# Who takes the low parts of sixteen weight chunks during a bit search: the vector engine or GpSimd

## Chip, cores and metric

One core of one Trainium2 chip. The metric is the device time of one execution in microseconds (us). Engines are named as in the profile: PE is TensorE (matmul), PEld its weight load, DVE the vector engine, ACT the scalar engine, POOL is GpSimd, SP is SyncE, which here issues most DMAs.

## What is computed

One step of a decoder layer for 272 prompt tokens (16 learned ones and 256) and 32 sample tokens (8 sequences of 4). The model is 2048 wide. The part of the reference that matters here is the sparse attention of the sample tokens: an indexer scores all 2048 + 4 past keys, and each query attends only to its best 256.

```python
h = einsum('btd,de->bte', x, w_in)          # q, k, v, iq, ik, iw, p
score = sum_h w[t,h] * relu(iq[t,h] . ik[s])
_, idx = lax.top_k(score, 256)              # per query
a = softmax(q . k[idx]) v[idx]
m = pooled(p) @ w_pool * pool_scale
x = layer_norm(ALPHA * x + concat(a, m) @ w_out)
f = (silu(gate) * val) @ w_down             # gate, val: conv of x @ w_up
y = layer_norm(ALPHA * x + f)
```

Everything is float32. The output must keep float32's accuracy and, above all, the same keys must be chosen.

## The kernel before, in words

**Weights as chunks, each in two parts.** All weights stream through three slots of 128x1024 float32 (`RING = 3`, 512 KB a chunk), in 354 chunks. For each chunk n: SP loads it into `raw` (`load_chunk`, L330 to L350) once `lo_done` says that the chunk three before it has been split; ACT rounds it to the matmul's reduced format, `w_hi = raw` (`hi`, L1012 to L1018), once TensorE is through with the chunk three before (`chunk_used`); then `w_lo = raw - w_hi` is formed (`lo`, L1348 to L1353) by DVE, and TensorE does three products for each 128x128 block, hi*x_hi, hi*x_lo and lo*x_hi (L459 to L461), 24 matmuls a chunk. `hi_done`, `lo_done` and `chunk_used` are counters: each chunk adds one, in order.

**The order of the work is written out by hand.** The stretch in question is a loop of 32 steps, one for each chunk KS + i (KS = 26), i = 0 to 31, which every engine's program goes through in its own way. The chunks are the projections to k, p and v. While TensorE multiplies chunk KS + i, ACT and DVE prepare chunk KS + i + 2, and each engine puts other work into the step:

- TensorE (L629 to L687): the chunk; in steps 4 to 7 the prompt's index scores (`prompt_index`); the sample scores against the cached keys, `sample_scores` (L609), one unit of four pages in most steps, two in steps 12, 15, 18 and on; and `total` (L588 to L593), a matmul with a 0/1 matrix that sums a count over partitions. In steps 4 to 19 `total` stands twice in each step: ahead of the last quarter of the chunk's matmuls ("mid"), and at the end of the step.
- DVE (L1560 to L1648): in steps 4 to 19 the search for the threshold. All 544 scores of each partition lie in `sc`. A candidate's bits are settled from the top down, 32 of them: `count` (L1505 to L1508) counts the scores at or over the candidate in one instruction with an accumulator, TensorE's `total` sums the counts, and `next_bit` (L1510 to L1516) sets the candidate anew in three instructions on 128x1, the last of them `cand = cand xor flip_i` (L1516). One round of this at a time can be under way. Two rounds go into each step, and between them stood `lo(KS + 2 + i)`.
- Also on DVE: `index_head` (L1489 to L1499), the weighted sum over the prompt's index heads, two heads in each of the steps 4 to 7 (four instructions with two tensor inputs); `rope_key` in steps 9, 11, 13 and 15 (a shuffle and three products, L1359 to L1362), each behind the second count of its step.
- ACT (L1109 to L1150): `hi(KS + 2 + i)` at the head of each step, then relus, evictions and score copies.
- SP (L384 to L407): the chunk load, then one or two units of cached keys (four loads of 256 KB each), which wait for `k_used`.
- GpSimd (L944 to L966): at the start memsets and 80 loads of cached index keys, the last at about 80 us; then it waits for `p_acc` (the last `index_head`) and masks the prompt's scores with three `affine_select` (L962), which `prompt_top` reads in steps 28 and on; then it issues half of the value loads (L966), the first at about 290 us. Between 80 and 290 us it has nothing else.

**Behind the search**, in step 20, DVE splits chunk KS + 22 and finishes the mask (L1598 to L1609); TensorE waits there for one more count (L634).

Of the kernel before, what the change touches and what calls it, by code (L numbers as in the profile page):

```python
# [37 lines left out]
KS, PS, VS = 26, 34, 50  # L38
# [34 lines left out]
def slot_of(n):  # L73

    return n % RING
# [22 lines left out]
def layer(nc, xT, w_iq, w_ik, w_in, w_out, w_up, w_down, kT_cache, v_cache, ik_cache, pages,  # L98
# [3 lines left out]
    f32, f32r, i32 = mybir.dt.float32, mybir.dt.float32r, mybir.dt.int32  # L102
    ALU, ACT, AX = mybir.AluOpType, mybir.ActivationFunctionType, mybir.AxisListType
# [9 lines left out]
    def put(name, shape, dt=f32, where=None):  # L113
        if where is None:
            where = region(4 * int(np.prod(shape[1:])))
        return nc.alloc_sbuf_tensor_at(name, shape, dt, offset=where)
# [9 lines left out]
    raw = put("raw", [128, RING, CK * CW])  # L126
    w_hi = put("w_hi", [128, RING, CK * CW], f32r)
    w_lo = put("w_lo", [128, RING, CK * CW], f32r)
# [88 lines left out]
    with ExitStack() as ctx:  # L217
# [3 lines left out]
        def sem(name):  # L221
            return ctx.enter_context(nc.semaphore(name))
# [12 lines left out]
        hi_done, lo_done, chunk_used = sem("hi_done"), sem("lo_done"), sem("chunk_used")  # L235
# [45 lines left out]
        def page_numbers(engine, first):  # L281

            return nc.values_load_multi_w_load_instructions(pt_sb[0:1, first:first + UNIT], engines=[engine],  # L283
                                                            min_val=0, max_val=NPHYS - 1)[1]
# [658 lines left out]
        @block.gpsimd  # L943
        def _(pool):  # L944
            PL = mybir.EngineType.Pool
            pool.memset(ones[:], 1.0).then_inc(preset, 1)
            pool.memset(tiny[:], EPS).then_inc(preset, 1)
            pool.memset(sc[:], NEG).then_inc(preset, 1)
            pool.memset(cand[:], 2.0).then_inc(preset, 1)
            pool.memset(q_pad[:], 0.0).then_inc(preset, 1)  # L950
            pool.memset(p_score[:, 0:64], 0.0).then_inc(preset, 1)
            pool.wait_ge(pages_in, 16)
            for g, b in [(0, b) for b in range(DB)] + [(1, 0), (1, 1)]:
                for j in range(2):
                    for i, r in enumerate(page_numbers(PL, NPG * b + 8 * j + 4 * g)):
                        pool.dma_start((ik_a, ik_b)[g][64 * j:64 * j + 64, b, i, :],
                                       ik_cache[bass.ds(r, 1)].rearrange("a p n -> p (a n)")).then_inc(ik_in[2 * g], 16)
            pool.wait_ge(p_acc, IH)
            pool.wait_ge(preset, 6)
            for i, (t0, n, keys, col) in enumerate(PQ):  # L960
                view = p_score[0:n, col:col + keys]
                pool.affine_select(out=view, in_=view, pattern=[[-1, keys]], compare_op=ALU.is_ge,  # L962
                                   fill=NEG if i else -FAR, base=t0, channel_multiplier=1).then_inc(p_causal, 1)

            for u in range(1, 32, 2):
                load_value_unit(pool, PL, u)  # L966

            def centre(z, tmp, blocks, round_):

                pool.wait_ge(mean_kept, round_ + 1)  # L970
                for k in blocks:
                    pool.tensor_tensor(z[:, k], z[:, k], tmp[:, 0], ALU.subtract).then_inc(centred, 1)  # L972

            centre(z1[:, :, M0:T], ln_a, CENTRE[0], 0)
            pool.wait_ge(x1_lo, KB)
            pool.wait_ge(rows_out, 32)
            pool.wait_ge(v_out, 16)
            pool.wait_ge(p_out, 16)
            for i in range(NUP):

                for a in range(2):
                    if i:
                        pool.wait_ge(conv_v, i * 4)
                    pool.wait_ge(conv_in, 32)
                    src = c_state[:, 2 * i + FB * a:2 * i + FB * a + 2, 0:16].rearrange("p j (b w) -> p j b w", w=2)
                    dst = u_ext[:, 2 * a:2 * a + 2, PT:PT + 6 * DB].rearrange("p j (b w) -> p j b w", w=6)
                    pool.tensor_copy(dst[:, :, :, 0:2], src).then_inc(ctx_put, 1)  # L987

                flat = c_state[:].rearrange("p j w -> p (j w)")
                for a in range(2):  # L990
                    pool.wait_ge(g_free, i * 4 + (4 * SL_UP + 2 * a + 2))
                    pool.wait_ge(ctx_put, i * 2 + 2)
                    dst = flat[:, i * 36 + 18 * FB * a:i * 36 + 18 * FB * a + 36].rearrange("p (j b w) -> p j b w", b=9, w=2)
                    src = u_ext[:, 2 * a:2 * a + 2, PT - 2:PT + 52].rearrange("p j (b w) -> p j b w", w=6)
                    pool.tensor_copy(dst, src[:, :, :, 0:2]).then_inc(tail_put, 1)  # L995

            pool.wait_ge(h_split, 2 * NUP)
            pool.wait_ge(tail_put, 2 * NUP)
            for k in range(KB):
                pool.tensor_tensor(z2[:, k], x_hi[:, k, META:T].bitcast(f32), x_lo[:, k, META:T].bitcast(f32),  # L1000
                                   ALU.add).then_inc(residual, 1)
            centre(z2, ln_b, CENTRE[1], 1)
# [329 lines left out]
        def _(dve):  # L1332
# [15 lines left out]
            def lo(n):  # L1348
                c = slot_of(n)
                width = 8 * IKW if IK0 <= n < Q0 else CK * CW  # L1350
                dve.wait_ge(hi_done, n + 1)
                dve.tensor_tensor(w_lo[:, c, 0:width], raw[:, c, 0:width], w_hi[:, c, 0:width].bitcast(f32),  # L1352
                                  ALU.subtract).then_inc(lo_done, 1)  # L1353
# [24 lines left out]
            def rope_key(j):  # L1378
                dve.wait_ge(g_free, 4 * SL_K + j + 1)
                if j:  # L1380
                    dve.wait_ge(k_roped, j)
                rope(k_t[0:32, j], rope_q, partner_q, k_roped)
# [177 lines left out]
            for i in range(32):  # L1560
# [17 lines left out]
                if 4 <= i < 20:  # L1578
                    it = 1 + 2 * (i - 4)
                    if it > 1:  # L1580
                        next_bit(32 - it)
                    count(cand[:], ALU.is_ge, it)
                    lo(KS + 2 + i)
                    next_bit(31 - it)
                    if it < 31:
                        count(cand[:], ALU.is_ge, it + 1)
                    else:
                        then(dve.tensor_scalar(sc[:], sc[:], sign, None, ALU.mult))
                        then(dve.tensor_scalar(thr, cand[:], sign, None, ALU.mult))
                        count(thr, ALU.is_gt, 32)  # L1590
# [2 lines left out]
                    index_head(2 * (i - 4) + 1)  # L1593
                if i in (9, 11, 13, 15):
                    rope_key((i - 9) // 2)
                if i >= 20:
                    lo(KS + 2 + i)
                if i == 20:  # L1598
# [246 lines left out]
            for s in range(NDN):  # L1845
                end = DN0 + DNC * (s + 1)
                for n in range(done, min(end + 2, END)):
                    lo(n)
                    c = n - DN0 - DNC
# [116 lines left out]
```

## Time and profile before

| | |
|---|---|
| median of 3 runs | 1372.3 us (1371.9, 1372.3, 1377.79) |
| the profiled execution's own time | 1376.97 us |
| its span on the core | 1375.3 us |
| PE busy | 1329.3 us, 97% |
| DVE busy | 772.4 us, 56% |
| ACT busy | 599.3 us, 44% |
| POOL busy | 169.5 us, 12% |
| mean granted clock of TensorE | 0.989 |

The profiled execution is one of the slower ones shown: its time lies 4.7 us over the median. Busy times and spans are those of that one execution. A matmul's end is modelled in the profile, so a busy PE is not PE at its peak. The clock is given as a share of 2.4 GHz. A wait for several semaphores is put down to the one that came last. Idle time of an engine costs nothing where another one sets the pace.

### The profile page before, as it was taken

To read this page: it belongs to the slowest core of one execution; us is meant where nothing else is said; L and a number is where in the kernel's file an instruction comes from. 1 tells how busy PE (TensorE), PEld (TensorE's weight loads), DVE (VectorE), ACT (ScalarE), POOL (GpSimd) and SP (SyncE) were. 2 spreads that over 40 slices of the span, in tenths; PEclk is the share of its full clock that TensorE was granted. 3 is DMA by queue.
4 is the path that set the end of the run, shared out by engine and by line. 5 is a ranking of instruction groups with operands and counts; after the bars stand their busy time and mean duration, and the time that the engine had idled before them with its cause. 6 is when DMAs were issued, how large, how long until landed. Compare 5 with 4: busy or idle time off the path is not lost.

```text
span 1375.3 us, 25589 instructions
## 1 busy us (share of the span) xinstructions
PE 1329.3 (97%) x9824; PEld 1225.8 (89%) x9824; DVE 772.4 (56%) x1291; ACT 599.3 (44%) x964; POOL 169.5 (12%) x286
## 2 busy tenths in 40 slices
PE   6999998999999999999999999999999999999995
PEld 6977776677677989999999999999999999999995
DVE  4645877766444766565565565565565535443434
ACT  3343312343333367554554554554554433333434
POOL 5510000012230040010010010010010500000002
PEclk9999999999999999999999999999999999999998
DMA  9656789989987536556555555555555655555552
GB/s 254 191 171 230 258 303 368 306 288 340 319 318 270 140 106 191 162 157 178 163 158 170 169 156 169 167 160 170 162 166 171 181 169 161 158 169 156 166 162 76
DMA packets 97421, 272.70 MB, mean 198 GB/s; under 512 B 13097, under 2 KB 19570, under 8 KB 97042
## 3 DMA queue, kind: packets, MB, share of 16 engines
q1 hardware_dynamic: 89618, 251.65, 59.1%
q0 software_dynamic: 7680, 19.41, 4.2%
q8 instruction: 77, 1.26, 0.4%
q14 instruction: 46, 0.38, 0.1%
HBM read 265.83 MB, written 5.18 MB: 197 GB/s over the span
## 4 chain that ended last, share of the span: by engine, by line
PE 82%; DMA 5%; SPq 5%; DVE 4%; issue 3%; ACT 1%; POOLq 0%; ACTq 0%; DVEq 0%; POOL 0%
PE G L459 25%; PE G L460 24%; PE G L461 24%; DMA raw<-in_w_in 2%; PE A L778 2%; SPq L283 1%; SPq L298 1%; PE A L609 1%; SPq L376 1%; DVE w_lo L1352 1%; DMA raw<-in_w_iq 1%; DMA raw<-in_w_out 1%; DMA k_ring<-in_kT_cache 1%; ACT w_hi L1018 1%; DMA v_ring_x<-in_v_cache 1%
## 5 line engine op out<-in xcount | busy, mean ns | idle before, releaser
L1352 DVE TENSOR_TENSOR w_lo<-raw,w_hi 128x1024 fp32r<-128x1024 f32 x354 | 434.9, 1229 | 451.9 <-ACT w_hi L1018 450.8
L1018 ACT ACTIVATE w_hi<-raw 128x1024 fp32r<-128x1024 f32 x354 | 373.9, 1056 | 566.1 <-PE G L461 459.1
L459 PE MATMUL G<-x_hi,w_hi 128*128 128x290 f32 (+1 forms) x1856 | 560.0, 302 | 17.7 <-DVE w_lo L1352 14.0
L460 PE MATMUL G<-x_lo,w_hi 128*128 128x290 f32 (+1 forms) x1856 | 554.3, 299 | 0.0
L461 PE MATMUL G<-x_hi,w_lo 128*128 128x290 f32 (+1 forms) x1856 | 550.9, 297 | 0.0
L459 PEld LDWEIGHTS G<-x_hi,w_hi 128*128 128x128 f32 x1856 | 351.4, 189 | 27.8 <-issue 21.5
L460 PEld LDWEIGHTS G<-x_lo,w_hi 128*128 128x128 f32 x1856 | 353.2, 190 | 0.2
L461 PEld LDWEIGHTS G<-x_hi,w_lo 128*128 128x128 f32 x1856 | 351.0, 189 | 0.0
L461 PE MATMUL G<-h_hi,w_lo 128*128 128x288 f32 x704 | 208.7, 296 | 0.0
L459 PE MATMUL G<-h_hi,w_hi 128*128 128x288 f32 x704 | 208.6, 296 | 0.0
L460 PE MATMUL G<-h_lo,w_hi 128*128 128x288 f32 x704 | 205.3, 292 | 0.0
L460 PEld LDWEIGHTS G<-h_lo,w_hi 128*128 128x128 f32 x704 | 134.2, 191 | 0.1
L459 PEld LDWEIGHTS G<-h_hi,w_hi 128*128 128x128 f32 x704 | 132.2, 188 | 1.4 <-issue 1.4
L461 PEld LDWEIGHTS G<-h_hi,w_lo 128*128 128x128 f32 x704 | 131.9, 187 | 0.0
L1806 DVE SCALAR_TENSOR_TENSOR conv<-u_ext,cp_sb,conv 128x304 f32<-128x304 f32 x176 | 90.2, 533 | 44.1 <-ACT conv L1303 40.9
L995 POOL COPY c_state<-u_ext 128x36 f32<-128x36 f32 x44 | 11.4, 260 | 369.3 <-ACT u_ext L1291 369.2
L987 POOL COPY u_ext<-c_state 128x32 f32<-128x32 f32 x44 | 39.4, 926 | 135.8 <-DVE conv L1806 118.6
L1303 ACT ACTIVATE conv<-u_ext,cp_sb 128x304 f32<-128x304 f32 x88 | 51.5, 638 | 0.0
L1290 ACT ACTIVATE u_ext<-G 128x258 f32<-128x258 f32 x88 | 33.7, 383 | 16.8 <-PE G L461 14.2
L972 POOL TENSOR_TENSOR z<-z,ln_b 128x288 f32<-128x288 f32 x10 | 8.7, 904 | 262.3 <-ACT ln_b L1257 262.3
L459 PE MATMUL G<-a_hi,w_hi 128*128 128x290 f32 x128 | 38.7, 302 | 2.3 <-DVE z L1798 1.4
L459 PE MATMUL G<-m_hi,w_hi 128*128 128x290 f32 x128 | 40.3, 315 | 0.0
(293 smaller groups left out, 1172.4 us busy)
## 6 DMA issues: line engine op xcount, KB each, us to landing
raw<-in_w_up SPq DMA_DIRECT2D x176, 512.0 KB, 3.6
raw<-in_w_down SPq DMA_DIRECT2D x88, 512.0 KB, 3.6
k_ring<-in_kT_cache SPq DMA_DIRECT2D x128, 256.0 KB, 4.1
raw<-in_w_in SPq DMA_DIRECT2D x48, 512.0 KB, 5.7
raw<-in_w_out SPq DMA_DIRECT2D x32, 512.0 KB, 5.4
v_ring_x<-in_v_cache POOLq DMA_DIRECT2D x44, 256.0 KB, 5.7
v_ring_p<-in_v_cache SPq DMA_DIRECT2D x32, 256.0 KB, 5.0
v_ring_x<-in_v_cache SPq DMA_DIRECT2D x28, 256.0 KB, 4.5
```

Source lines behind the costliest of these rows:

```text
L283: return nc.values_load_multi_w_load_instructions(pt_sb[0:1, first:first + UNIT], engines=[engine], min_val=0, max_val=NPHYS - 1)[1]
L298: eng.dma_start(k_ring[:, UNIT * (u % 4) + i, :], kT_cache[bass.ds(r, 1)].rearrange("a p n -> p (a n)")).then_inc(k_in[u % 4], 16)
L459: pe.matmul(out, hi, xh, start=start, stop=False)
L460: pe.matmul(out, hi, xl, start=False, stop=False)
L461: return pe.matmul(out, lo, xh, start=False, stop=stop)
L778: mm = pe.matmul(A[32 * i:32 * i + 32, 2, :], p_tok[:, b // 4, b % 4, UNIT * u + i, :], value_slot(w, i), start=u == 0, stop=u == 3)
L987: pool.tensor_copy(dst[:, :, :, 0:2], src).then_inc(ctx_put, 1)
L1018: act.activation(w_hi[:, c, 0:width], raw[:, c, 0:width], ACT.Copy).then_inc(hi_done, 1)
L1290: act.activation(u_ext[:, j, 0:PT], G[:, j, 0:PT], ACT.Copy).then_inc(act_own, 1)
L1303: act.activation(conv[:, j, 0:UO], u_ext[:, j, 0:UO], ACT.Identity, scale=cp_sb[:, t, 0:1], bias=cp_sb[:, t, 3:4]).then_inc(conv_a, 1)
L1352: dve.tensor_tensor(w_lo[:, c, 0:width], raw[:, c, 0:width], w_hi[:, c, 0:width].bitcast(f32), ALU.subtract).then_inc(lo_done, 1)
L1806: return dve.scalar_tensor_tensor(out=conv[:, j, 0:UO], in0=u_ext[:, j, w:w + UO], scalar=cp_sb[:, t, w:w + 1], in1=conv[:, j, 0:UO], op0= ...
```

## The change

GpSimd forms w_lo of chunks KS + 6 to KS + 21, those that DVE formed in steps 4 to 19. It does so in one run behind its loads of index keys and ahead of the masking of the prompt's scores; each split waits for its w_hi alone, the first also for the six splits before it by DVE, so that `lo_done` counts in order. In step 20 DVE waits for all of GpSimd's splits before its own next one.

```diff
@@ gpsimd
                         pool.dma_start((ik_a, ik_b)[g][64 * j:64 * j + 64, b, i, :],
                                        ik_cache[bass.ds(r, 1)].rearrange("a p n -> p (a n)")).then_inc(ik_in[2 * g], 16)
+            for n in range(KS + 6, KS + 22):
+                c = slot_of(n)
+                if n == KS + 6:
+                    pool.wait_ge(lo_done, n)
+                pool.wait_ge(hi_done, n + 1)
+                pool.tensor_tensor(w_lo[:, c, :], raw[:, c, :], w_hi[:, c, :].bitcast(f32), ALU.subtract).then_inc(lo_done, 1)
             pool.wait_ge(p_acc, IH)
             pool.wait_ge(preset, 6)
@@ vector, steps 4 to 19
                     count(cand[:], ALU.is_ge, it)
-                    lo(KS + 2 + i)
                     next_bit(31 - it)
@@ vector
                     rope_key((i - 9) // 2)
+                if i == 20:
+                    dve.wait_ge(lo_done, KS + 22)
                 if i >= 20:
                     lo(KS + 2 + i)
```

## Rows read from the trace of the kernel before

**Rows 1.** The page: busy us of an engine, share of the span, instructions.
```profile
PE 1329.3 (97%) x9824; PEld 1225.8 (89%) x9824; DVE 772.4 (56%) x1291; ACT 599.3 (44%) x964; POOL 169.5 (12%) x286
```

**Rows 2.** Busy time by stretch: busy us of each engine, granted clock, DMA.
```profile
136.00:236.00 100.00, 91.66 (x647) 70.95 (x647) 77.98 (x221) 26.57 (x41) 0.88 (x3) 0.98 0.86 304
...
184.40:188.40 4.00, 4.00 (x19) 4.00 (x20) 3.76 (x10) 1.06 (x1) 0.00 (x0) 0.58 1.05 388
...
236.00:240.00 4.00, 4.00 (x34) 2.31 (x34) 3.11 (x5) 0.43 (x1) 0.00 (x0) 0.57 1.02 383
...
236.00:400.00 164.00, 162.88 (x1157) 116.15 (x1160) 95.19 (x247) 58.62 (x115) 27.93 (x52) 0.99 0.91 312
```

**Rows 3.** Who waited for whom, 137 to 234 us: total, times, longest.
```profile
PE A L593 <- DVE junk L1507: 5.6, 10, 2.4
```

**Rows 4.** Groups of DVE, 137.9 to 232 us: busy, mean ns, idle before.
```profile
L1507 DVE TENSOR_SCALAR_CACHE_REDUCE junk<-sc,cand 128x544 f32<-128x544 f32 x31 | 24.2, 779 | 1.1
L1352 DVE TENSOR_TENSOR w_lo<-raw,w_hi 128x1024 fp32r<-128x1024 f32 x16 | 19.6, 1225 | 7.0 <-ACT w_hi L1018 6.6
```

**Rows 5.** Timeline: start, us, engine and line, idle before and its releaser.
```profile
136.35 0.38 PE L593 MATMUL A<-sel_k,msum 128*128 128x1 f32 x2 [1.58 <-DVE junk L1507]
...
180.48 1.06 ACT L1018 ACTIVATE w_hi<-raw 128x1024 fp32r<-128x1024 f32 x1 [9.04 <-DMA raw<-in_w_in]
...
181.64 1.23 DVE L1352 TENSOR_TENSOR w_lo<-raw,w_hi 128x1024 fp32r<-128x1024 f32 x1 [2.91 <-ACT w_hi L1018]
...
184.25 0.38 PE L593 MATMUL A<-sel_k,msum 128*128 128x1 f32 x2 [2.40 <-DVE junk L1507]
...
235.73 0.38 PE L593 MATMUL A<-sel_k,lmat 128*128 128x1 f32 x2 [1.58 <-DVE sc L1601]
```

**Rows 6.** Timeline of step 6.
```profile
148.12 1.06 ACT L1018 ACTIVATE w_hi<-raw 128x1024 fp32r<-128x1024 f32 x1
...
149.95 0.16 DVE L1516 TENSOR_TENSOR cand<-cand,flip_i 128x1 int32<-128x1 int32 x1
...
150.99 0.38 PE L593 MATMUL A<-sel_k,msum 128*128 128x1 f32 x2
```

**Rows 7.** Timeline of step 10.
```profile
170.38 1.06 ACT L1018 ACTIVATE w_hi<-raw 128x1024 fp32r<-128x1024 f32 x1 [4.27 <-PE G L461]
...
171.87 0.46 DVE L1361 TENSOR_TENSOR k_t<-k_t,rope_q 32x304 f32<-32x304 f32 x1
...
174.21 0.38 PE L593 MATMUL A<-sel_k,msum 128*128 128x1 f32 x2
```

**Rows 8.** Timeline of steps 13 and 17.
```profile
189.93 1.06 ACT L1018 ACTIVATE w_hi<-raw 128x1024 fp32r<-128x1024 f32 x1 [4.43 <-PE G L461]
...
192.55 0.16 DVE L1516 TENSOR_TENSOR cand<-cand,flip_i 128x1 int32<-128x1 int32 x1
...
214.43 1.06 ACT L1018 ACTIVATE w_hi<-raw 128x1024 fp32r<-128x1024 f32 x1 [3.31 <-DMA raw<-in_w_in]
...
216.05 0.16 DVE L1516 TENSOR_TENSOR cand<-cand,flip_i 128x1 int32<-128x1 int32 x1
...
217.96 0.28 PE L593 MATMUL A<-sel_k,msum 128*128 128x1 f32 x2
```

**Rows 9.** Timeline where GpSimd and DVE meet.
```profile
161.87 0.88 POOL L962 TENSOR_SCALAR_AFFINE_SELECT p_score<-p_score 50x64 f32<-50x64 f32 x3 [82.48 <-DVE p_score L1498]
...
161.98 0.78 DVE L1516 TENSOR_TENSOR cand<-cand,flip_i 128x1 int32<-128x1 int32 x1
...
1080.78 1.34 DVE L1352 TENSOR_TENSOR w_lo<-raw,w_hi 128x1024 fp32r<-128x1024 f32 x1 [0.63 <-ACT w_hi L1018]
```

**Rows 10.** One line's instructions: duration ns least/median/most, first and last start.
```profile
L1000 POOL TENSOR_TENSOR z<-x_hi,x_lo x16: 805/816/1812, 1080.2 to 1096.6; 128x288 f32<-128x288 f32 x16
...
L995 POOL COPY c_state<-u_ext x44: 213/216/313, 532.6 to 1070.6; 128x36 f32<-128x36 f32 x44
...
L1460 DVE MAX8 top<-p_score x2: 324/379/434, 289.0 to 310.7; 104x8 f32<-104x168 f32 x1, 104x8 f32<-104x272 f32 x1
```

## The prediction

> **What bounds the kernel now.** I read the page first: TensorE is busy 97% of the span [rows 1]. So a change on the vector engine pays only where TensorE waits for it. Next the busy time by stretch: over 136 to 236 us, where the 32 bits of the threshold are searched, TensorE is busy 91.66 of 100 us, DVE 77.98 and GpSimd 0.88; right after its two longest idle times there are 4 us at a granted clock of 0.58 and 0.57, the lower level of 1.2 GHz [rows 2]. The waits put 5.6 us of that idle time on the count of the search (L593 behind L1507) [rows 3]; the timeline shows its largest piece, 2.40 us at 184.25, because the vector engine sat 2.91 us in front of the split w_lo until ACT had made w_hi and only then came back to the search, and behind it 1.58 us more at 235.73, in step 20, after DVE's split of chunk 48 [rows 5]. Together 7.2 us.
>
> The search is a ring: DVE counts (L1507, 779 ns [rows 4]), TensorE sums over partitions (L593), DVE flips the bit in three small instructions, the last of them cand = cand xor flip_i (L1516). It goes round twice in each step i = 4 to 19: TensorE asks for one count in front of the last quarter of the chunk ("mid") and one at the end of the step.
>
> **The change, part by part.** *Removed from DVE:* sixteen splits of 1225 ns, 19.6 us [rows 4], and DVE's waits for w_hi in front of them. They lie beside TensorE's work, except where TensorE then waits. Most that can come back is those 7.2 us and the two slow stretches. Their price: 4 us at 0.58 lose 0.42 x 4 = 1.7 us, 3.4 for both [rows 2]. Ceiling: 7.2 + 3.4 = **10.6 us**.
>
> *Added on GpSimd:* sixteen splits of 128x1024. The trace has no such size. Nearest rows: two-input operations of 128x288, least 805, median 816 ns [rows 10]. In proportion that is 1024/288 x 816 = 2.90 us, the upper end; taking 213 ns of it as fixed, what GpSimd's copies of 36 elements need at least [rows 10], leaves 603/288 = 2.1 ns an element, so 213 + 1024 x 2.1 = 2.36. I take **2.45 us**, nearer to the second, since a large operation has its fixed part once, and keep 2.2 to 2.9. The Trainium skill (GPSIMD Engine Reference, "Elementwise — side-by-side cycle accounting") gives 4497 ns for 2048 elements, by which a split would be an estimated 2.25 us and the sum some 2 us smaller; no run here shows that size. GpSimd has room: 2.45 us in a step of some 6, and TensorE uses a chunk two steps after its w_hi. So w_lo is not late itself, and the raw slots, freed by lo_done, come free no later than now: today DVE splits after its first count. Cost of that: nothing, covered by two steps of lead; without the cover 1.2 us a chunk. GpSimd's queue: the three affine selects move from 161.87 to behind the last split, about 230; their first reader starts at 289.0 [rows 10], so 59 us cover them. The value loads behind them wait for k_used and stay where they are. No DMA moves; SP's waits are on the same counts. The added DVE wait at step 20 is for work done before w_hi of chunk 48, for which DVE waits anyway.
>
> *What it puts in the way: the lock.* At 161.87 GpSimd ran three selects in 0.88 us, up to 162.75. DVE's cand, which takes 159 ns otherwise, started at 161.98 and took 0.78, up to 162.76 [rows 9]. So DVE's tiny two-input operation waited until GpSimd was done. The same at 1080.78: w_lo took 1.34 us beside a run of GpSimd's two-input operations [rows 9], and of these, 816 ns by the median, one took 1812 [rows 10]: held in its turn. The Trainium skill (SBUF — State Buffer, "SBUF: two separate sides") has the rule: whichever comes first, GpSimd or a DVE operation with two SBUF inputs, holds the shared ports for its whole instruction. The trace agrees. Counting itself has one tensor input, and at 779 ns for 544 elements I take it to run beside GpSimd; no row here shows that overlap.
>
> So each GpSimd split is a closed window for cand, for the three products of a rope, and for the index heads. It opens 1.16 us after w_hi starts (DVE's own split began so much after it at 181.64 against 180.48, [rows 5]) and lasts 2.45. Against each step's ring:
>
> - *Steps 5 to 7, behind the index heads.* Step 6: w_hi at 148.12, window 149.3 (149.6 behind the running head) to 152.05. cand stood at 149.95, is held 2.1 us, and the count with it; TensorE wanted it at 150.99, when it was just done [rows 6]. Stall 2.0 us. Step 5 has its copy at the same place, 1.7. In step 7 the copy comes later against the ring and window and cand meet in the same tenth: a coin's throw, 0 or 2.4, so 1.2. Sum **4.9**; ends 0 and 7.2.
> - *Steps 10, 12, 14, 16, behind a rope.* Step 10: w_hi at 170.38, window 171.5 to 174.3 (GpSimd first waits out the rope's first product, already running). The product of 171.87 is held to 174.3, 2.4 us, and so is the count behind it, which TensorE asks for at 174.21 and gets without a wait [rows 7]. Stall 2.4 us; step 14 has the same places. In 12 and 16 the raw chunk lands late and the window lies differently: 1.3 each, half-way. Sum **7.4**; ends 3 and 9.6.
> - *Eight other steps* (in step 4 the search has hardly begun: 0). Step 13: w_hi at 189.93, window to 193.5, cand from 192.55 to 193.5, count done at 194.5, about when asked: 0. Step 17: w_hi at 214.43, window to 218.05, cand from 216.05 held 2.0, slack 0.9: 1.1 [rows 8]. Most are nearer to step 13; mean 0.25, sum **2.0**; ends 0 and 8.
>
> New idle time: 4.9 + 7.4 + 2.0 = **14.3 us**. Five of these stalls are over 1.5 us (steps 5, 6, 10, 14 and one of 12 and 16). Of the three such idle times now (1.58 us before 136.35, 2.40, 1.58) two were followed by a slow stretch [rows 2, 5], so 3.3 more at 1.7 us: **5.6 us**. Removed: 10.6, the one at 235.73 with it, since TensorE arrives later and the transfers catch up. Sum: 14.3 + 5.6 - 10.6 = **+9 us**. Behind the search TensorE is busy 162.88 of 164 us [rows 2], so there is no idle time left to take it up, and it stays to the end.
>
> The sum is made against the profiled execution (span 1375.3, its time 1376.97), 4.7 us above the median of 1372.3, so I add the difference to the median: 1372.3 + 9 = **1381 us**.
>
> **The rivals.**
>
> *The search only gets free.* If cand and the ropes ran beside GpSimd, all 10.6 us come back: 1362. For it: DVE is alone in 16 steps, and the 2.40 us wait is plainly the split's. Against: [rows 9]. A softer form: the window falls where DVE is waiting for TensorE. Chance 0.13.
>
> *A draw.* The search slides in the ring until cand falls before or after the window. Stalls are then half of mine, 7.1, with one slow stretch, 1.7; less 10.6 is -1.8: 1370.5; with two thirds of the stalls and two stretches, 9.5 + 3.4 - 10.6, +2: 1374.5. Call it 1373. For it: in 8 of 15 steps the window already falls so, and w_hi starts with TensorE's last matmul, so a late TensorE moves the window too. Chance 0.25.
>
> *Forecast.* 1376 to 1387, chance 0.49.
>
> *Longer windows.* GpSimd needs 2.9 us, and every stall is followed by a slow stretch. Ten held steps at 0.45 more, 4.5; five stretches, 8.5; less only 7.3, since the wait at 235.73 and its slow stretch stay: 14.3 + 4.5 + 8.5 - 7.3 = +20: 1392. Chance 0.13.
>
> **How the numbers follow.** About 0.5%, 6.9 us, is what a measurement of this kernel can tell from no change: 1365.4 to 1379.2. Faster: the first rival and a sliver of the second, 0.14. Same: most of the draw and the forecast's lower edge, 0.33. Slower: 0.53. Range, leaving out the full first rival and the tail of the last: 1367 to 1390.
>
> **What would show it.** In the changed profile: GpSimd's splits at 2.2 to 2.9 us, and some at over 3 where DVE held the ports first; cand with a median of 159 ns but several of 1 to 2.5 us, and rope products likewise; TensorE's idle time in front of L593 at 10 to 18 us, largest in steps 5, 6, 10 and 14; more stretches at the lower clock; no wait for w_lo from GpSimd. I am wrong if L1516 stays near 159 ns throughout, if the idle time in front of L593 falls below 5 us, or if chunks of weights are late for TensorE.

## The result: slower by 1.4%, the direction that was forecast, and twice as much

| | before | after |
|---|---|---|
| median | 1375.05 us (4 runs, 1371.9 to 1377.87) | 1393.32 us (4 runs, 1389.14 to 1398.99) |
| the profiled execution's own time / span | 1376.97 / 1375.3 us | 1394.63 / 1392.9 us |
| search stage, from the first count's total to the first matmul of L650 in step 20 | 102.9 us | 117.4 us |
| TensorE idle in front of the count in that stage | 7.2 us | 14.7 us |
| mean granted clock of the whole span | 0.989 | 0.987 |

The ratio of the runs is 1.0136, with a 95% interval of 1.0088 to 1.0184: slower by 12 to 25 us. Measured again later, beside other kernels, it was 1.0165 (1.0140 to 1.0189). The forecast was 1381 us, +9, in a range of 1367 to 1390: the sign holds, the forecast size is half of the measured one, and the value lies 3 us outside the range. Both bounds of the interval are clear of no change.

The lines of the changed kernel have moved: the split on DVE is L1358, `count` L1513, the flips L1519 to L1522, the rope L1365 to L1368, w_hi L1024, and GpSimd's split is L963. TensorE's lines are the same.

The profile's page and its busy time by stretch, to be laid beside [rows 1, 2] (columns: PE, PEld, DVE, ACT and POOL busy us, granted clock, DMA share, GB/s):

```profile
PE 1337.4 (96%) x9824; PEld 1229.0 (88%) x9824; DVE 772.8 (55%) x1275; ACT 599.4 (43%) x964; POOL 209.8 (15%) x302
```

```profile
136.00:236.00 100.00, 84.10 (x535) 63.17 (x536) 68.12 (x178) 22.78 (x37) 34.63 (x14) 0.90 0.72 251
164.00:171.00 7.00, 6.07 (x27) 5.01 (x26) 3.73 (x12) 3.17 (x7) 1.59 (x1) 0.51 0.82 301
185.00:189.00 4.00, 4.00 (x17) 2.03 (x17) 1.32 (x5) 1.06 (x1) 0.63 (x1) 0.50 1.04 404
201.00:205.00 4.00, 4.00 (x21) 1.15 (x20) 0.93 (x3) 1.06 (x1) 2.36 (x1) 0.58 0.47 174
215.00:219.00 4.00, 4.00 (x19) 2.03 (x19) 1.32 (x5) 0.13 (x1) 0.00 (x0) 0.57 1.00 379
```

Read the first one as a whole: in the same 100 us TensorE does 535 matmuls in place of 647, at a clock of 0.90. DVE lost sixteen splits of 1.2 us, and yet its busy time over the whole span is the same as before, 772.8 against 772.4 us. That is the first sign: something else on DVE grew by as much as was taken off. The four short stretches are at or near the lower clock of 1.2 GHz, and TensorE is busy in nearly all of them (6.07 of 7 us, and 4.00 of 4 three times): it waits for nothing there, it is only slower.

The groups of DVE from 138.4 to 247 us say what grew (busy us, mean ns of one, idle before):

```profile
L1513 DVE TENSOR_SCALAR_CACHE_REDUCE junk<-sc,cand 128x544 f32<-128x544 f32 x31 | 24.2, 779 | 1.1
L1522 DVE TENSOR_TENSOR cand<-cand,flip_i 128x1 int32<-128x1 int32 x31 | 18.0, 580 | 1.1
L1367 DVE TENSOR_TENSOR k_t<-k_t,rope_q 32x304 f32<-32x304 f32 x4 | 8.1, 2029 | 0.1
```

The count takes 779 ns as before, in all 31 places. cand, an operation on one number for each partition, takes 580 ns in the mean instead of 179, and one product of the rope 2029 instead of 462. Together that is 12.5 + 6.3 = 18.8 us more, against 19.6 us of splits less. The instructions of one line, with least, median and most, show that it is a few long ones and not a slower engine, and what GpSimd's split really takes:

```profile
L1522 DVE TENSOR_TENSOR cand<-cand,flip_i x31: 159/160/2255, 140.4 to 247.0; 128x1 int32<-128x1 int32 x31
```

```profile
L963 POOL TENSOR_TENSOR w_lo<-raw,w_hi x16: 2357/2385/2705, 137.9 to 242.9; 128x1024 fp32r<-128x1024 f32 x16
```

The timeline of step 6 is the whole mechanism in seven rows; the place is that of [rows 6]:

```profile
150.20 1.06 ACT L1024 ACTIVATE w_hi<-raw 128x1024 fp32r<-128x1024 f32 x1
...
151.34 2.58 POOL L963 TENSOR_TENSOR w_lo<-raw,w_hi 128x1024 fp32r<-128x1024 f32 x1 [5.17 <-ACT w_hi L1024]
151.60 0.21 DVE L1519 TENSOR_SCALAR flip_i<-A,sel_k 128x1 int32<-128x1 f32 x1
151.85 0.15 DVE L1521 TENSOR_SCALAR flip_i<-flip_i 128x1 int32<-128x1 int32 x1
...
152.03 1.90 DVE L1522 TENSOR_TENSOR cand<-cand,flip_i 128x1 int32<-128x1 int32 x1
153.97 0.78 DVE L1513 TENSOR_SCALAR_CACHE_REDUCE junk<-sc,cand 128x544 f32<-128x544 f32 x1
...
154.81 0.38 PE L593 MATMUL A<-sel_k,msum 128*128 128x1 f32 x2 [1.58 <-DVE junk L1513]
```

w_hi starts at 150.20, GpSimd's split 1.14 us later, and it ends at 151.34 + 2.58 = 153.92. DVE's two flips with one SBUF input run beside it at their usual 0.21 and 0.15 us. cand has two and ends at 152.03 + 1.90 = 153.93, together with the split. The time in which an instruction is held counts as busy in the profile: that is why DVE's busy time has not fallen. In step 10, behind the first rope, the same for a product ([rows 7]):

```profile
179.97 2.65 POOL L963 TENSOR_TENSOR w_lo<-raw,w_hi 128x1024 fp32r<-128x1024 f32 x1 [3.46 <-ACT w_hi L1024]
180.38 2.56 DVE L1367 TENSOR_TENSOR k_t<-k_t,rope_q 32x304 f32<-32x304 f32 x1
```

Steps 14 and 16 look the same. In step 12 the rope is through before the split starts, and it is cand that is held, until 199.17:

```profile
196.80 2.36 POOL L963 TENSOR_TENSOR w_lo<-raw,w_hi 128x1024 fp32r<-128x1024 f32 x1 [6.06 <-ACT w_hi L1024]
197.07 2.10 DVE L1522 TENSOR_TENSOR cand<-cand,flip_i 128x1 int32<-128x1 int32 x1
```

TensorE then waits at the mid count, in steps 5, 6 and 7 (behind the index heads) and 10, 12, 14 and 16 (with a rope in front of the count). From the timeline, all of over 1 us behind the first count; step 6 stands above:

```profile
147.05 0.38 PE L593 MATMUL A<-sel_k,msum 128*128 128x1 f32 x2 [1.37 <-DVE junk L1513]
...
163.01 0.38 PE L593 MATMUL A<-sel_k,msum 128*128 128x1 f32 x2 [2.03 <-DVE junk L1513]
...
184.83 0.59 PE L593 MATMUL A<-sel_k,msum 128*128 128x1 f32 x2 [2.17 <-DVE junk L1513]
...
200.05 0.38 PE L593 MATMUL A<-sel_k,msum 128*128 128x1 f32 x2 [2.02 <-DVE junk L1513]
...
214.94 0.38 PE L593 MATMUL A<-sel_k,msum 128*128 128x1 f32 x2 [2.17 <-DVE junk L1513]
...
229.23 0.38 PE L593 MATMUL A<-sel_k,msum 128*128 128x1 f32 x2 [1.65 <-DVE junk L1513]
```

With the smaller ones that is 14.7 us. No matmul waits for w_lo from GpSimd.

**Where the 17.6 us of the two profiled spans are.** 14.5 lie between the first count and L650. Of them 14.7 - 7.2 = 7.5 are idle time in front of the count. 6.8 are the clock: summing what is missing to full clock over each microsecond of the stage gives 10.24 us after and 3.41 before, and it comes in equal pieces of 1.71 us, one for each stretch of 4 us at half clock: six against two (the stretches of 164 to 171 and 184 to 192 us count as two each). 0.4 us lie ahead of the stage, 2.7 behind it, in pieces that differ from one execution to the next: over all profiles here the half clock behind the stage costs between some 6 and some 14 us, in no order that goes by the kernel.

### The profile page after: what moved, and what is told of

The parts are those of the page before. It is cut to its first block, busy times and chain, and to the rows that moved or that the text cites. A ratio compares the mean times of both kernels' runs of the same rounds, so it can differ in the third digit from the quotient of the medians.

```text
span 1392.9 us, 25590 instructions
## 1 busy us (share of the span) xinstructions
PE 1337.4 (96%) x9824; PEld 1229.0 (88%) x9824; DVE 772.8 (55%) x1275; ACT 599.4 (43%) x964; POOL 209.8 (15%) x302
## 4 chain that ended last, share of the span: by engine, by line
PE 82%; DVE 6%; DMA 4%; SPq 4%; issue 3%; ACT 1%; POOLq 0%; ACTq 0%; DVEq 0%; POOL 0%
PE G L459 24%; PE G L460 24%; PE G L461 24%; PE A L778 2%; DMA raw<-in_w_in 1%; PE A L609 1%; SPq L376 1%; DVE cand L1522 1%; SPq L283 1%; DMA raw<-in_w_out 1%; DMA k_ring<-in_kT_cache 1%; ACT w_hi L1024 1%; DMA raw<-in_w_iq 1%; DVE junk L1513 1%; DVE w_lo L1358 1%
## 5 line engine op out<-in xcount | busy, mean ns | idle before, releaser
L1358 DVE TENSOR_TENSOR w_lo<-raw,w_hi 128x1024 fp32r<-128x1024 f32 x338 | 415.4, 1229 | 443.7 <-ACT w_hi L1024 443.0
L1024 ACT ACTIVATE w_hi<-raw 128x1024 fp32r<-128x1024 f32 x354 | 373.8, 1056 | 560.3 <-PE G L461 476.7
L963 POOL TENSOR_TENSOR w_lo<-raw,w_hi 128x1024 fp32r<-128x1024 f32 x16 | 39.4, 2462 | 126.4 <-ACT w_hi L1024 126.4
L593 PEld LDWEIGHTS A<-sel_k,msum 128*128 128x128 f32 x66 | 10.8, 203 | 35.3 <-DVE junk L1513 27.1
```

The lines of the kernel that those rows point to most:

```text
L963: pool.tensor_tensor(w_lo[:, c, :], raw[:, c, :], w_hi[:, c, :].bitcast(f32), ALU.subtract).then_inc(lo_done, 1)
L1024: act.activation(w_hi[:, c, 0:width], raw[:, c, 0:width], ACT.Copy).then_inc(hi_done, 1)
```

## The experiments

All ratios are to the kernel before, measured beside it on the same chip, with the 95% interval. "Stage" is as in the table above; idle is TensorE's in front of the count within it; slow is what half clock cost within it, by the same sum. Both are of one profiled execution.

| kernel | ratio | stage | idle | slow |
|---|---|---|---|---|
| before | 1 | 102.9 | 7.2 | 3.4 |
| changed | 1.0136 (1.0088 to 1.0184) | 117.4 | 14.7 | 10.2 |
| changed, again | 1.0165 (1.0140 to 1.0189) | 115.9 | 16.2 | 6.8 |
| cand in PSUM | 1.0035 (1.0009 to 1.0061) | 108.0 | 7.6 | 8.5 |
| cand and ropes in PSUM | 0.9978 (0.9957 to 1.0000) | 95.8 | 3.4 | 0 |
| the same, again | 0.9967 (0.9952 to 0.9982) | 97.7 | 5.0 | 0 |
| before, with the same PSUM paths | 1.0003 (0.9980 to 1.0025) | 98.7 | 6.0 | 0 |
| nobody splits | 0.9957 (0.9934 to 0.9980) | 96.4 | 2.1 | 1.7 |
| waits filled | 1.0138 (1.0089 to 1.0187) | 110.8 | 6.5 | 1.7 |
| waits filled, again | 1.0137 (1.0114 to 1.0160) | 111.2 | 8.1 | 0 |
| split in halves | 1.0081 (1.0059 to 1.0103) | 106.6 | 9.9 | 3.4 |
| seven splits | 1.0023 (1.0002 to 1.0044) | 101.7 | 7.0 | 1.7 |
| twelve splits, cand in PSUM | 0.9980 (0.9962 to 0.9998) | 98.9 | 5.8 | 0 |

### cand with one SBUF input

```diff
+            flip = A[:, 3, 1:2].bitcast(i32)
...
-                then(dve.tensor_scalar(flip_i[:], tot, need, float(2 ** b), ALU.is_lt, ALU.mult))
+                then(dve.tensor_scalar(flip, tot, need, float(2 ** b), ALU.is_lt, ALU.mult))
...
-                then(dve.tensor_tensor(cand[:].bitcast(i32), cand[:].bitcast(i32), flip_i[:], ALU.bitwise_xor))
+                then(dve.tensor_tensor(cand[:].bitcast(i32), cand[:].bitcast(i32), flip, ALU.bitwise_xor))
```

> The changed kernel with one thing moved: flip_i, and with it the third instruction of the bit step, reads its flip from PSUM, so cand = cand xor flip has one SBUF input in place of two. Same instruction count, same GpSimd splits. Theory L (a DVE instruction with two SBUF inputs is held until GpSimd's running split ends): cand is at 0.2 to 0.3 us in all 31 places (it had up to 2.26 us), the stalls ahead of the mid count in steps 5, 6, 9 and 17 (1.4, 1.6, 0.6, 0.6 us) shrink to under 0.3, those behind a rope (2.2, 2.0, 2.2, 1.6 us in steps 10, 12, 14, 16) stay. TensorE's idle time in front of the count falls from 16 us to 8 to 11, and the kernel is at 1.005 to 1.011 of the one before (the changed kernel: 1.0136). Rival O (DVE is held by GpSimd whatever its operands are, or slowed by GpSimd's memory traffic): cand keeps spans of 1 to 2 us and nothing moves, 1.0136. Rival W (w_lo from GpSimd comes late, or the order of the queues does it): nothing moves either, but with cand at 0.2.

The line's instructions, and the waits of over 1 us that are left behind the first count:

```profile
L1523 DVE TENSOR_TENSOR cand<-cand,A x31: 154/155/156, 142.0 to 236.3; 128x1 int32<-128x1 int32 x31
```

```profile
179.23 0.58 PE L593 MATMUL A<-sel_k,msum 128*128 128x1 f32 x2 [2.20 <-DVE junk L1514]
...
205.79 0.38 PE L593 MATMUL A<-sel_k,msum 128*128 128x1 f32 x2 [2.20 <-DVE junk L1514]
...
219.78 0.38 PE L593 MATMUL A<-sel_k,msum 128*128 128x1 f32 x2 [1.37 <-DVE junk L1514]
```

cand is at 154 to 156 ns in all 31 places; nothing else was moved, and GpSimd's splits still run. The stalls of steps 5, 6, 7, 9 and 17 are gone, those of steps 10, 14 and 16 stay. The ratio of 1.0035 and the idle time of 7.6 us both lie just under what was expected (1.005 to 1.011, 8 to 11 us). Theory O (held whatever the operands) and theory W (w_lo late) are out. A part of what it gained beyond the forecast shows in step 12: its stall was put down to the rope, but it was cand that was held there (197.07 above), and with its operand in PSUM this stall goes too. Of the 8.5 us of half clock 3.4 lie at 138 to 145 us, behind the wait in front of the first count, which this run doesn't change.

### cand and ropes

This is the edit of cand above and, beside it, the four key ropes of the search:

```diff
-                rope(k_t[0:32, j], rope_q, partner_q, k_roped)
+                x, part = k_t[0:32, j], A[0:32, 2, 0:T]
+                then(dve.stream_shuffle(part, x, partner_q))
+                then(dve.tensor_tensor(swap[0:32, 0:T], part, rope_q[0:32, 1], ALU.mult))
+                then(dve.tensor_copy(part, x))
+                then(dve.tensor_tensor(part, part, rope_q[0:32, 0], ALU.mult))
+                dve.tensor_tensor(x, part, swap[0:32, 0:T], ALU.add).then_inc(k_roped, 1)
```

> As the run with cand in PSUM, and the four key ropes of the search also go through a PSUM bank, so that none of their products has two SBUF inputs (one more instruction for each rope, some 0.4 us of DVE). Theory L: the stalls of steps 10, 12, 14 and 16 go as well; what is left is the index heads of steps 5 to 7 (up to 2 us each). Idle time in front of the count 3 to 5 us, three to four stretches of half clock fewer than in the changed kernel, ratio 0.996 to 1.003. Rivals O and W: 1.01 or over, rope products keep spans of over 2 us (O).

> The kernel with GpSimd's sixteen splits and with cand and the key ropes in PSUM, once more beside its control without GpSimd. It was at 0.9978 (0.9957 to 1.0000). Theory L: 0.996 to 1.000, and below its control by 0.2 to 0.5%, which is what the change is worth once nothing on DVE's path is held. Rival P: same as the control within 0.1%.

> The kernel before (all splits on DVE) with cand's flip and the four key ropes going through PSUM, as in the run that came out at 0.998 with GpSimd's splits. A control. Theory L: PSUM operands help only against GpSimd's windows; here there are none, so nothing is gained and 0.4 us of DVE work is added for each rope, ratio 0.999 to 1.003. Rival P (the PSUM path itself is faster, or spares DVE something else): ratio 0.996 or lower, and the gains of the two PSUM runs say nothing on the lock.

The first two are one kernel: 0.9978 and 0.9967. No wait of the search is over 1.5 us, no stretch is at half clock. cand in the middle of a split, in the second of the runs:

```profile
144.54 2.40 POOL L963 TENSOR_TENSOR w_lo<-raw,w_hi 128x1024 fp32r<-128x1024 f32 x1 [5.45 <-ACT w_hi L1024]
144.62 0.22 DVE L1525 TENSOR_SCALAR A<-A,sel_k 128x1 int32<-128x1 f32 x1
144.87 0.17 DVE L1527 TENSOR_SCALAR A<-A 128x1 int32<-128x1 int32 x1
145.07 0.15 DVE L1528 TENSOR_TENSOR cand<-cand,A 128x1 int32<-128x1 int32 x1
145.26 0.78 DVE L1519 TENSOR_SCALAR_CACHE_REDUCE junk<-sc,cand 128x544 f32<-128x544 f32 x1
```

The whole ring step, count included, runs inside GpSimd's 2.40 us without loss. The index heads, which still read two SBUF tensors and of which up to 2 us each had been feared, bring no stall in steps 5 to 7. The control, the kernel before with the same PSUM paths and no GpSimd split, is at 1.0003: PSUM gives nothing by itself that these runs could tell (0.2% either way), it takes DVE out of GpSimd's way. In its profile too the stage has no slow stretch and is 4 us shorter than that of the kernel before, and its runs are still no faster: a stage of one profiled execution differs by a few us from the median's, and ratios decide here. Between the control at 1376.58 and the PSUM kernel beside it at 1371.39 us lie 5.2 us (0.2 to 0.5% were expected): what moving the splits is worth once cand and the ropes are not held. Measured against the kernel before, this version is the fastest of all that compute everything, by 0.3%.

Something on DVE's path is still held, and it is no instruction with two tensors: the sign's product `sc = sc * sign` (L1589, L1583 in the changed kernel) and the line L1599 in step 20, each 128x544 with one tensor input and a scalar for each partition. Alone they take 0.50 us. In the second of these runs:

```profile
136.71 2.38 POOL L963 TENSOR_TENSOR w_lo<-raw,w_hi 128x1024 fp32r<-128x1024 f32 x1 [57.24 <-ACT w_hi L1024]
137.42 1.98 DVE L1589 TENSOR_SCALAR sc<-sc,sel_k 128x544 f32<-128x544 f32 x1
...
224.29 2.38 POOL L963 TENSOR_TENSOR w_lo<-raw,w_hi 128x1024 fp32r<-128x1024 f32 x1 [1.57 <-ACT w_hi L1024]
225.29 1.68 DVE L1599 TENSOR_SCALAR sc<-sc,sel_k 128x544 f32<-128x544 f32 x1
...
228.09 0.38 PE L593 MATMUL A<-sel_k,msum 128*128 128x1 f32 x2 [1.43 <-DVE junk L1519]
```

Both end 0.3 us behind the split, and behind them come two of this run's largest waits, 0.93 us at 140.28 and 1.43 at 228.09. The sign's product took 2.0 to 2.6 us in six of the profiles with GpSimd's splits and 0.50 to 0.52 in the others, where it started ahead of the first split or fell between two halves of it. The count, with the same tensor, never took over 0.79. So a single tensor input is no safe conduct by itself; what sets these two apart from the count no run here tests.

### Nobody splits

```diff
-                pool.tensor_tensor(w_lo[:, c, :], raw[:, c, :], w_hi[:, c, :].bitcast(f32), ALU.subtract).then_inc(lo_done, 1)
+                pool.nop().then_inc(lo_done, 1)
```

> The changed kernel without the subtraction: GpSimd only waits for w_hi and counts lo_done up, so nobody forms the low parts of these sixteen chunks (TensorE multiplies with what the slot held). It prices what the search gains when it is freed of the split and nothing takes its place. Theory L: all stalls ahead of the mid counts go, idle time in front of the count 0 to 2 us, ratio 0.990 to 0.996 (the 7.2 us of idle time and 3.4 us of half clock of the kernel before come back). Rival D (removing DVE's split is itself what hurts, by letting other work collide, for instance transfers that start earlier): ratio over 1.0. Rival W: as fast as theory L says, since w_lo is never late here; the two are told apart by the run with cand in PSUM.

This leaves out the low parts of sixteen chunks. 0.9957 (0.9934 to 0.9980): a search freed of its splits is worth 5.9 us, at most 9.1, not the 10.6 of the ceiling. What stays is mostly in step 20, nearly the 1.58 us of before the change [rows 5]:

```profile
230.28 0.38 PE L593 MATMUL A<-sel_k,lmat 128*128 128x1 f32 x2 [1.47 <-DVE sc L1608]
```

The kernel with PSUM paths, measured beside it, is at 0.9978, within 0.2% of this floor, and the intervals overlap.

### The waits filled with matmuls

```diff
+            def filled_total(it, count):
+
+                if count:
+                    pe.wait_ge(p_relu, min(it - 1, IH))
+                for _ in range(count):
+                    pe.matmul(A[:, 2, 128:256], ones[:], ones[:], start=True, stop=True)
+                total(it, msum)
...
+                fill_mm = {5: 4, 6: 5, 7: 6, 10: 7, 12: 6, 14: 7, 16: 5}.get(i, 0)
```

> The changed kernel with 4 to 7 dummy matmuls (128x128, into an idle PSUM bank) in front of the mid count in the seven steps with stalls of 1.4 to 2.2 us (5, 6, 7, 10, 12, 14, 16), about as much work as each stall is long. DVE's and GpSimd's work is as in the changed kernel. Theory C (a large part of the loss is the half clock behind each stall, not the stall): the granted clock over 136 to 254 us rises from 0.91 to 0.98 or more, the search stage gets 5 to 8 us shorter although nothing waits less, ratio 1.006 to 1.010. Rival (the stalls alone set it): ratio 1.0136 or a little over.

> The kernel with dummy matmuls in the waits again. Its profile had the search stage 6.5 us shorter than the changed kernel's and one half-clock stretch there in place of six, but its median over four runs was no better, with two stretches later on. Theory C (the half clock behind the stalls is a real part of the loss): with more runs 1.006 to 1.010, at least 0.3% below the changed kernel of this call. Rival (the slow stretches only move to a later place, so their number in an execution is what it is): within 0.2% of the changed kernel of this call.

> The changed kernel itself, once more, beside the others of this call. 1.0136 in its first measurement with an interval of 0.5% each way; 1.011 to 1.016 now. In the profile the idle time in front of the count is again 14 to 16 us, since the windows and the waits are fixed by the order of the queues; the number of half-clock stretches of 4 us in the search may differ (six in the first profile).

The stage of the second of these runs and that of the changed kernel beside it:

```profile
137.00:248.00 111.00, 101.75 (x755) 79.65 (x754) 82.64 (x205) 25.81 (x41) 39.62 (x19) 1.00 0.81 278
```

```profile
137.00:254.00 117.00, 99.84 (x681) 75.36 (x682) 83.65 (x209) 26.96 (x43) 39.98 (x19) 0.94 0.77 263
```

In the stage it is as theory C says: DVE and GpSimd work as slowly as in the changed kernel, TensorE waits for the same counts, and yet the stage is 4.7 us shorter (111.2 against 115.9), because its clock stays at 1.00 in place of 0.94. Of the whole time it brought less: 1.0138 and 1.0137 where 1.006 to 1.010 was expected. Beside the changed kernel it is 0.3% faster, 1392.78 against 1397.22 us, or 4.1 us (1.7 to 6.5) by the means of six and five executions; the first time, at 1.0138 against the 1.0136 of another measurement, no gain was seen.

How much of the clock reaches the end can be read from all executions, since each has its span and mean granted clock: (1 - clock) x span is the time lost to the throttle. For the profiles of these three kernels this comes within 1 us of the sum over microseconds.

| means | time | lost to the clock | the rest |
|---|---|---|---|
| before (17 executions) | 1375.2 | 11.6 | 1363.6 |
| changed, again (5) | 1396.8 | 23.4 | 1373.4 |
| waits filled, again (6) | 1392.7 | 16.0 | 1376.7 |

So of the changed kernel's 21.7 us some 12 are the clock and some 10 everything else, each to within 2.2. Filling the waits gives 7.4 us of clock back over the whole execution, and 3.4 are lost again elsewhere: the forty dummy matmuls of the stage (eighty in the profile's count, 10.0 us in all) are more work than the 8.1 us of waiting that they replace. What the clock takes is not in the stage alone: both profiles lose 5.1 us to half clock long behind the search, the filled kernel's at 436 to 446 us and the changed one's at 443 to 453.

The changed kernel itself came out at 1.0165 and 16.2 us of idle time, both a little over what was expected (1.011 to 1.016, 14 to 16). The one wait that was not there the first time, 1.52 us in step 4, stands behind the sign's product, held for 2.56 us at 138.14.

### The split in halves

```diff
-                pool.tensor_tensor(w_lo[:, c, :], raw[:, c, :], w_hi[:, c, :].bitcast(f32), ALU.subtract).then_inc(lo_done, 1)
+                for h in range(2):
+                    o = slice(CW * h, CW * h + CW)
+                    ins = pool.tensor_tensor(w_lo[:, c, o], raw[:, c, o], w_hi[:, c, o].bitcast(f32), ALU.subtract)
+                ins.then_inc(lo_done, 1)
```

> The changed kernel with every GpSimd split cut into two instructions on 128x512 each (the second counts lo_done). Same elements, same order, one more instruction for each. Theory L (the shared ports are held for one whole GpSimd instruction, and go to DVE between two): a DVE instruction is held 1.2 to 1.3 us at most in place of 2.3 to 2.6, so cand at most 1.3 us, stalls ahead of the mid counts 0.2 to 1.1 us instead of 1.4 to 2.2, idle time in front of the count 5 to 9 us, fewer slow stretches, ratio 1.003 to 1.008. Rival (DVE is held until GpSimd has run out of queued work): the same holds as in the changed kernel or a little longer, since both halves are queued at once, ratio 1.0136 or over.

The two halves and the rope in step 10:

```profile
174.03 3.02 POOL L965 TENSOR_TENSOR w_lo<-raw,w_hi 128x512 fp32r<-128x512 f32 x2 [3.00 <-ACT w_hi L1027]
174.45 1.45 DVE L1370 TENSOR_TENSOR k_t<-k_t,rope_q 32x304 f32<-32x304 f32 x1
175.94 1.44 DVE L1371 TENSOR_TENSOR k_t<-k_t,swap 32x304 f32<-32x304 f32 x1
...
178.76 0.38 PE L593 MATMUL A<-sel_k,msum 128*128 128x1 f32 x2 [2.05 <-DVE junk L1516]
```

Held for one GpSimd instruction, not until its queue is empty: between the halves DVE gets in, does its product (174.45 + 1.45), and the second half is pushed back in turn. cand was held 1.2 us at most, and the stalls of steps 5 to 7 fell from 1.4, 1.6 and 2.0 us to 0.3, 0.5 and 0.9. Behind three of the ropes nothing is won, 2.05, 2.04 and 1.74 us in steps 10, 14 and 16: in step 10 two products stand in a row, and each meets one half. In step 12, where cand was held, 2.0 fell to 0.95. 1.0081 is just over the upper edge of what was expected (1.008), and the idle time of 9.9 us is over its 9; that step I had not thought through.

### Fewer splits on GpSimd

```diff
+POOL_LO = tuple(KS + 2 + i for i in (4, 8, 11, 13, 15, 18, 19))
...
                     count(cand[:], ALU.is_ge, it)
+                    if KS + 2 + i not in POOL_LO:
+                        if KS + 1 + i in POOL_LO:
+                            dve.wait_ge(lo_done, KS + 2 + i)
+                        lo(KS + 2 + i)
                     next_bit(31 - it)
```

GpSimd's loop then goes over `POOL_LO` and waits for `lo_done` = n ahead of each of its splits. The second run has twelve numbers in `POOL_LO`, all but those of steps 10, 12, 14 and 16, and cand's flip in PSUM.

> GpSimd takes only the seven splits (steps 4, 8, 11, 13, 15, 18, 19) in whose step the changed kernel's profile has no stall ahead of the mid count; DVE keeps the other nine, right behind its first count as in the kernel before. Theory L: the windows of these seven lie beside nothing that has two SBUF inputs and is urgent, so no stall of over 1 us at the mid counts, at most one or two slow stretches, ratio 0.995 to 1.003. The two waits of the kernel before in front of a split (2.40 and 1.08 us, steps 11 and 15) go. Rival (GpSimd's splits cost in proportion to their number, 18 us for sixteen): seven of sixteen give 1.006.

> cand's flip in PSUM; GpSimd takes twelve splits, DVE keeps those of steps 10, 12, 14 and 16, behind the ropes, which stay in SBUF. Theory L: nothing urgent with two SBUF inputs meets a window, except the index heads of steps 5 to 7, which were harmless with cand in PSUM, and the last product of a rope if GpSimd's split of the step before still runs (one stall of 2.2 us, as in the run with seven splits, step 12). Idle time in front of the count 3 to 5 us, ratio 0.994 to 1.000. Rival: the splits that DVE keeps bring the waits for w_hi back, ratio over 1.0.

Seven splits in SBUF: 1.0023, in the range, but not without stalls. They were chosen as harmless from the changed kernel's profile, and the choice didn't hold, since the windows moved with the rest. In step 11 w_hi came late, behind its transfer, and the window fell on the rope's last product:

```profile
183.92 2.59 POOL L964 TENSOR_TENSOR w_lo<-raw,w_hi 128x1024 fp32r<-128x1024 f32 x1 [17.29 <-ACT w_hi L1025]
184.29 2.54 DVE L1369 TENSOR_TENSOR k_t<-k_t,swap 32x304 f32<-32x304 f32 x1
...
188.22 0.38 PE L595 MATMUL A<-sel_k,msum 128*128 128x1 f32 x2 [2.17 <-DVE junk L1514]
```

Twelve splits with cand in PSUM: 0.9980, with that one stall of 2.19 us again, as expected; the idle time of 5.8 us is over the 3 to 5 expected, by the 1.19 us in step 4 behind the sign's product. A loss in proportion to the number of splits is out: seven would cost 0.6% and cost 0.2% (at most 0.44), and twelve cost nothing.

## Why the prediction was wrong in size and right in kind

- **The lock.** Right. From one place of the trace before, where cand took 0.78 us beside three selects [rows 9], the same follows for every window that cand met: it ends with the split (153.93 and 153.92), and with a PSUM operand it isn't held at all. The expectation that counting runs beside GpSimd, which no row showed, holds too: 778 to 781 ns in 31 places. One instruction was overlooked: the sign's product in step 4, for which the prediction had put nothing, has one tensor input and was held all the same in six profiles; in the first profile of the changed kernel it started ahead of the split and wasn't.
- **GpSimd's split.** 2.45 us taken, 2.385 by the median; five of the sixteen took 2.58 to 2.71, each started while a long DVE instruction was running (an index head, the rope's first product, the sign's product). Over 3 us, which was named as a sign, none took. The proportional end, 2.9, fell away, and with it that part of the rival of longer windows. The estimate from the Trainium skill (GPSIMD Engine Reference, "Elementwise — side-by-side cycle accounting"), 2.25 us, was 0.13 too low.
- **The new stalls.** 14.3 us taken, 14.7 measured. Index heads 4.9 against 1.4 + 1.6 + 2.0 = 5.0; ropes 7.4 against 2.2 + 2.0 + 2.2 + 1.7 = 8.0; the others 2.0 against 0.6 + 0.6 + 0.3 + 0.3 = 1.7. That the sum fits is in part luck: steps 12 and 16 were 2.0 and 1.7 in place of 1.3 each and step 7 was 2.0 in place of 1.2, while steps 5, 6, 10 and 14 came out 0.2 to 0.4 us under what was taken. The half-way value for 12 and 16 took the late chunks of the kernel before, which were in time with TensorE later, and in step 12 cand was held and not the rope.
- **The idle time removed.** 7.2 taken; none of the old places is left in the changed kernel. But as a ceiling it was too high: with nobody splitting 2.1 us of waits stay and the kernel gains 5.9 us, not 10.6. By this the rival of a freed search would have given 1372.3 - 5.9, some 1366, not 1362.
- **The clock: the step that failed.** "3.3 more at 1.7 us: 5.6 us", less 3.4. The price of one was right, 1.71 us in every stretch. Their number was wrong: six in place of 3.3, net 6.8 us in place of 2.2. The share of two in three even held in this profile: of six waits of over 1.5 us (five were forecast) four were followed by half clock, all but those ahead of 154.81 and 229.23. But I took each to cost one stretch, and two of the four cost two back to back (164 to 171, and 184 to 192). A share from three cases should have carried its upper end into the range: every one of the five stalls followed is 8.5 us in place of the 5.6 of the sum, and with a stretch and a half for each of the six waits it is 9 x 1.71 = 15. The executions of the second measurement say the same without a profile: the clock took 11.9 us more than before where the sum had 5.6 - 3.4 = 2.2, and everything else 9.8 where it had 14.3 - 7.2 = 7.1. So the clock is nearly 10 of the 12 us that were missing there.
- **"It stays to the end."** It stays and is joined by 2.7 us more: a wait of 0.75 us in step 22 for the masks of DVE, and what changes from execution to execution. No run here says what of this is the change's. The two measurements, +18 and +22 us, agree within their intervals.
- **The rivals.** The draw failed at its own point: cand did not slide out of the windows. As I read the order of the queues, w_hi, which opens the window, and cand hang on the same end of the same chunk, so a later TensorE moves both alike; no run tests this. The rival of longer windows gave the nearest time, 1392, but not for its reasons: the split takes 2.385 us and not 2.9, and not every stall was followed by half clock; its five new stretches and the one left over make the six measured only because two of them were doubled.

## What to carry over

Before work is moved from DVE to GpSimd, look at which instructions on DVE read two SBUF tensors, however small they are, and whether any of them stands in a ring with a third engine (and at those with one tensor that run as fast as the sign's product, 128x544 in 0.50 us); a wait that is counted as busy doesn't show in DVE's sum. If there are such, give one of their operands a place in PSUM first, and the move pays (0.9967 here). Where TensorE is near its limit, price a stall of some 2 us at nearly twice its length: of the waits of 2 us and more in these profiles twelve of fifteen were followed by 1.7 us of half clock or twice that. Read the granted clock of every execution and not of the profiled one alone.

## What the runs showed of the hardware that I had not expected

- GpSimd and DVE change places between two instructions even when GpSimd's next one is already queued: products of 1.45 and 1.44 us, one after each half.
- A DVE instruction with one tensor input can be held as well: `sc = sc * sign`, 0.50 us alone, took 2.0 to 2.6 beside a split, while the count of the same tensor stayed at 0.78.
- In the search stage half clock comes in pieces of one size, 4 us long and 1.71 us dear, sometimes two in a row, in every profile here that has any. Filling the waits with dummy matmuls left none of them in one profile (clock 1.00 in place of 0.94) and in the other only one at 137 to 141 us, ahead of the first filled wait.
- The longer the wait, the more often a slow stretch followed. Over all thirteen profiles it did behind twelve of the fifteen waits of 2.0 us and more in the stage (not behind one of 2.19 us with twelve splits, one of 2.04 with halves, and one of 2.02 in the changed kernel's second profile, where the first had one behind the same wait), behind two of the twelve of 1.3 to 1.8 us, and behind three of the thirteen of 1.56 to 1.58 us that stand in front of the first count in every profile. With the waits filled down to 0.2 to 1.1 us none followed. So the length of a wait alone doesn't decide it. What does is open.
